# Two edits in an RWKV-7 block: group norm between the last sample states, and the inverse's levels in 32-column diagonal blocks

## Chip, cores and metric

One core of one Trainium2 chip, one launch. The metric is the device time of that launch in microseconds, lower is better. The program is written engine by engine in a low-level language: each engine has its own instruction queue, and the queues wait for each other by semaphores.

## The reference, cut to what matters

The model has two layers over 256 prompt rows and 8 x 4 sample rows (288 rows of 1024). Layer 0 is a gMLP block with a dense SwiGLU; layer 1 is an RWKV-7 time mixing with a mixture of experts (8 experts, top 2). The change lies in the time mixing. Its recurrence and its group norm:

```python
def step(s, inp):
    r_t, w_t, k_t, v_t, kk_t, a_t = inp
    s_kk = jnp.einsum("bhij,bhj->bhi", s, kk_t)
    s = (s * w_t[:, :, None, :]
         - s_kk[..., None] * (kk_t * a_t)[:, :, None, :]
         + v_t[..., None] * k_t[:, :, None, :])
    y = jnp.einsum("bhij,bhj->bhi", s, r_t)
    return s, y
...
yc = y - jnp.mean(y, axis=-1, keepdims=True)
y = yc * lax.rsqrt(jnp.mean(yc * yc, axis=-1, keepdims=True) + GN_EPS)
y = y.reshape(bsz, t, D_MODEL) * lnx_g + lnx_b
bonus = jnp.sum(rh * kh * r_k, axis=-1, keepdims=True) * vh
y = (y + bonus.reshape(bsz, t, D_MODEL)).astype(h.dtype)
out = (y * g) @ w_out
```

There are 16 heads of 64 columns. All of it is float32.

## The kernel before, in words

The recurrence over the prompt is done in four chunks of 64 rows. Inside a chunk the rows depend on each other by a unit triangular matrix of 64 x 64 for each head; its inverse is needed. Two chunks share the 128 partitions (chunk pair `i` = 0 or 1, the second chunk in partitions 64 to 127), so one step works on 2 x 16 matrices.

**The inverse** (queue steps `xt0`, `x0`, `t1`, `xl`) doubles its diagonal blocks: level 0 by a masked copy (L1162), then levels m = 1 to 5 for blocks of 2, 4, 8, 16 and 32. `XT` holds the transposed inverse so far, `X` the inverse. `t1` (TensorE L1663) multiplies the matrix `MS[.., BL, ..]` by X, ScalarE copies the product to `T1` (L808); `xl` (L1678) multiplies XT by T1 both ways round, and VectorE copies the entries of the level under a mask `lvl` into X and XT (L1170, copy_predicated). Level 5 updates only XT. Each step works in two halves `f` of eight heads; each half has 16 matmuls of 64x64 (8 heads, 2 chunks), and an fp32 matmul is two pairs of LDWEIGHTS and MATMUL in the trace. The two chunks' matmuls lie in different tiles of the array: rows and columns 0 to 63, and 64 to 127.

**The chunks** then run in order, `w1`, `u`, `s`, `y` for c = 0 to 3. In `u` TensorE multiplies the inverse by W1 (L1724) and puts `key_value` or `y_value` (L1711, L1716) between, which are of the same 64x64 shape:

```python
for p in range(DC):
    mm = t.matmul(banks[2 + h2][cs, 64 * p:64 * p + 64], XT[cs, i, 2 * p + h2, :], W1[cs, h2, p, :],
                  start=(p == 0), stop=True, skip_group_check=True)
    ...
    other(p, 1 - e)
```

**The samples** (8 sequences of 4 rows) have steps with a name in `q_`: scores (L1767), their small inverse in one 32x32 tile (L1779, L1786, L1793), `q_s0` (states in, L1807), `q_qs` (L1816, 8 moving columns), `q_w1`, `q_u` (L1828, L1832, L1840), `q_y`, and `q_st(p)` (L1865, L1874), which makes the new state of two heads and hands it to ScalarE (L854) and a DMA. For `q_st(p + 2)` GpSimd spreads keys into blocks (L611), after `q_st(p)`.

**The order** is written out by hand in one list `steps`, which every engine walks through: `then(step)` appends a step of the prompt and behind it the next one of `fill`, the list of sample steps and of the scores of the second chunk pair. When the prompt's steps are over, what is left of `fill` follows: here `q_u(1)`, `q_y(1)`, `q_st(4)` to `q_st(7)`.

**Group norm** comes after the list. TensorE transposes the prompt's last state for the output; then for each of 8 chunks of channels c a matmul with `halves` gives the mean (L1888), VectorE subtracts it (L1219), ScalarE squares (L860). Then for each c: the variance by `halves` (L1897), the gate's two matmuls with `b_g2` in banks 6 and 7 (L1901 with 128 rows, L1902 with 32), the square root on ScalarE (L863), and on VectorE reciprocal (L1223), times gain (L1225), plus `b_lnx_b` plus bonus (L1228), times gate (L1232). The output projection (L1913) waits for all eight.

Of the kernel before, what the change touches and what calls it, by code (L numbers as in the profile page):

```python
# [54 lines left out]
def trunk_kernel(nc, a, out):  # L55

    with ExitStack() as ctx:
# [113 lines left out]
        ysq = tokens(B[8])  # L171
# [5 lines left out]
        XT = view(B[0], 2 * D, "p (i h t) -> p i h t", i=2, h=H)  # L177
        X = view(B[0] + 2048, D, "p (h t) -> p h t", h=H)
        T1 = view(B[0] + 3072, D, "p (f h t) -> p f h t", f=2, h=8)
# [6 lines left out]
        lvl = view(CHN + 5376, 768, "p (l x t) -> p l x t", l=6, x=2)  # L186
# [6 lines left out]
        id64 = view(CHN + 7200, 64)  # L193
        mskS = view(CHN + 7424, 2 * SMP, "p (r t) -> p r t", parts=2 * SMP, r=2)
# [13 lines left out]
        wkvo = view(CHN + 1024, 512, "p (c j) -> p c j", c=DC)  # L208
# [31 lines left out]
        for name in """const pool_order vec_in x_in ws_in wsS_in router_in vec_ready tr_ready xt_ready sq_ready  # L240
# [7 lines left out]
            gn_root g_ready yg_ready wo_ready r_const zero_out outg_in r_logit r_chain r_exp r_e r_sel r_pos r_most xtk_dve  # L248
# [116 lines left out]
        steps += fill  # L365
# [40 lines left out]
        def x_count(i, m, f, x):  # L406

            return 18 * i + 4 * (m - 1) + (2 * f + x if m < 5 else f) + 1
# [41 lines left out]
        def _(sp):  # L450
# [24 lines left out]
            for st in steps:  # L475
                if st == ("xl", 1, 5):
                    sp.wait_ge(S["t1_ready"], 20)
# [49 lines left out]
        def _(pool):  # L527
# [60 lines left out]
            step(g.tensor_tensor(lvl, lvlW[:, :, :, 0:64], lvlW[:, :, :, 64:128], ALU.add))  # L588
            step(g.tensor_tensor(id64, ident[:, 0:64], ident[:, 64:128], ALU.add))

# [13 lines left out]
            g.tensor_copy(XT, bc(id64, 1, [P, 2 * H, 64]).rearrange("p (i h) t -> p i h t", i=2)).then_inc(S["masks"], 1)  # L604
            pool.wait_ge(S["masks"], 2)
            g.tensor_copy(XTq[SB], bc(id64[SB, SMP:2 * SMP], 1, [SMP, H, SMP])).then_inc(S["masks"], 1)
# [9 lines left out]
            pool.wait_ge(S["masks"], 3)  # L616
            pool.wait_ge(S["sc_ready"], 16)
# [15 lines left out]
            pool.wait_ge(S["st_tr"], 1)  # L633
# [10 lines left out]
            for i in range(3):  # L644
# [7 lines left out]
                .then_inc(S["outg_in"], 16)  # L652
            pool.wait_ge(S["zero_out"], 16)
# [27 lines left out]
        def _(act):  # L681
# [25 lines left out]
            act.dma_start(router, a["m_router"][0].rearrange("(k p) e -> p k e", p=P)).then_inc(S["router_in"], 16)  # L707
# [87 lines left out]
            for st in steps:  # L795
                k = st[0]
                if k == "x0":
                    i = st[1]
                    for f in range(2):
                        act.wait_ge(S["xt_tr"], 2 * i + f + 1)  # L800
                        s_.activation(X[:, 8 * f:8 * f + 8, :], banks[1 + 3 * f][:, :].rearrange("p (h t) -> p h t", h=8),
                                      ACT.Copy).then_inc(S["x0_ready"], 1)
                elif k == "t1":
                    _, i, m = st
                    n = 5 * i + m - 1
                    for f in range(2):
                        act.wait_ge(S["t1_ready"], 2 * n + f + 1)
                        s_.activation(T1[:, f], banks[3 * f][:, :].rearrange("p (h t) -> p h t", h=8), ACT.Copy) \  # L808
                            .then_inc(S["t1_done"], 1)
# [46 lines left out]
            act.wait_ge(S["st_tr"], 1)  # L856
            s_.activation(wkvo, banks[0][:, :].rearrange("p (c j) -> p c j", c=DC), ACT.Copy).then_inc(S["st_row"], 1)
            for c in range(DC):
                act.wait_ge(S["gn_yc"], c + 1)
                s_.activation(ysq[:, c, :], yT[:, c, :], ACT.Square).then_inc(S["gn_sq"], 1)  # L860
            for c in range(DC):
                act.wait_ge(S["gn_var"], c + 1)
                s_.activation(t1T[:, c, :], banks[4 + c % 2][:, 0:T], ACT.Sqrt, bias=eps[:, 2:3], scale=1.0 / HD) \  # L863
                    .then_inc(S["gn_root"], 1)
# [81 lines left out]
        def _(dve):  # L946
# [49 lines left out]
            dve.wait_ge(S["rows_in"], 48)  # L996
# [147 lines left out]
            for c in range(DC):  # L1144
                dve.wait_ge(S["rb_ready"], c + 1)
                v.tensor_tensor(bonT[:, c, :], banks[BON[c]][:, 0:T], vfT[:, c, :], ALU.mult).then_inc(S["bon_ready"], 1)
            for st in steps:
# [9 lines left out]
                elif k == "xt0":  # L1157
# [3 lines left out]
                    for f in range(2):  # L1161
                        v.copy_predicated(XT[:, i, 8 * f:8 * f + 8, :], bc(lvl[:, 0, 1, :], 1, [P, 8, 64]).bitcast(I32),  # L1162
                                          MS[:, BL, i, 8 * f:8 * f + 8, :]).then_inc(S["xt0_ready"], 1)
                elif k == "xl":
                    _, i, m = st
                    for f in range(2):
                        for x in range(0 if m < 5 else 1, 2):
                            dve.wait_ge(S["x_ready"], x_count(i, m, f, x))
                            dst = XT[:, i, 8 * f:8 * f + 8, :] if x else X[:, 8 * f:8 * f + 8, :]
                            v.copy_predicated(dst, bc(lvl[:, m, x, :], 1, [P, 8, 64]).bitcast(I32),  # L1170
                                              banks[1 + 3 * f + x][:, :].rearrange("p (h t) -> p h t", h=8)) \
# [30 lines left out]
                elif k == "q_xt0":  # L1202
                    q_wait(dve, "q_ms", 1)
                    v.copy_predicated(XTq[SB], bc(lvl[SB, 0, 1, SB], 1, [SMP, H, SMP]).bitcast(I32), MSq[SB, :, 0, :]) \
                        .then_inc(S["q_dve"], 1)
                elif k == "q_x2":
                    g_ = st[1]
                    q_wait(dve, "q_x2", g_)
                    v.copy_predicated(XTq[SB, 8 * g_:8 * g_ + 8, :], bc(lvl[SB, 1, 1, SB], 1, [SMP, 8, SMP]).bitcast(I32),
                                      banks[7][SB, 0:256].rearrange("p (h t) -> p h t", h=8)).then_inc(S["q_dve"], 1)  # L1210
                elif k == "q_y":
# [3 lines left out]
                                    Qs[:, :, 1, :], ALU.add).then_inc(S["q_dve"], 1)  # L1215

            for c in range(DC):
                dve.wait_ge(S["gn_mean"], c + 1)
                v.scalar_tensor_tensor(out=yT[:, c, :], in0=banks[2 + c % 2][:, 0:T], scalar=-1.0 / HD, in1=yT[:, c, :],  # L1219
                                       op0=ALU.mult, op1=ALU.add).then_inc(S["gn_yc"], 1)  # L1220
            for c in range(DC):
# [8 lines left out]
                dve.wait_ge(S["r_chain"], 3 * c + 3)  # L1230
                dve.wait_ge(S["g_ready"], c + 1)
                v.tensor_tensor(yT[:, c, :], banks[6 + c % 2][:, 0:T], yT[:, c, :], ALU.mult).then_inc(S["yg_ready"], 1)  # L1232
# [4 lines left out]
            chain = [3 * DC]  # L1237
# [157 lines left out]
        def _(pe):  # L1395
# [218 lines left out]
            BOTH = (slice(0, 64), slice(64, 128))  # L1614

# [9 lines left out]
            for st in steps:  # L1625
# [19 lines left out]
                elif k == "x0":  # L1645
                    i = st[1]
                    for f in range(2):
                        pe.wait_ge(S["xt0_ready"], 2 * i + f + 1)
                        for j in range(8):
                            for ch in BOTH:  # L1650
                                mm = t.matmul(banks[1 + 3 * f][ch, 64 * j:64 * j + 64], XT[ch, i, 8 * f + j, :], id64[ch],
                                              start=(j == 0), stop=True, skip_group_check=True)
                        mm.then_inc(S["xt_tr"], 1)
                elif k == "t1":
                    _, i, m = st
                    for f in range(2):
# [9 lines left out]
                elif k == "xl":  # L1666
                    _, i, m = st
                    for f in range(2):
                        pe.wait_ge(S["t1_done"], 2 * (5 * i + m - 1) + f + 1)
                        if m > 1:  # L1670
                            pe.wait_ge(S["x_done"], x_count(i, m - 1, f, 1))
                        elif i:
                            pe.wait_ge(S["x_done"], x_count(0, 5, f, 1))
                        for x in range(0 if m < 5 else 1, 2):
                            for j in range(8):
                                for ch in BOTH:
# [3 lines left out]
                            mm.then_inc(S["x_ready"], 1)  # L1680
                elif k == "w1":
# [3 lines left out]
                    if c == 0:  # L1685
                        pe.wait_ge(S["x_done"], 36)
# [381 lines left out]
```

## Time and profile before

| what | value |
|---|---|
| median of 3 runs | 1684.76 us (1683.76 to 1685.39) |
| the profiled execution | 1685.16 us, its span 1683.3 us |
| TensorE matmul busy | 1588.4 us (94% of the span) |
| VectorE, ScalarE, GpSimd busy | 1030.5, 780.3, 88.4 us |
| inverse, first x0 to last xl | 621 to 697 us |
| chunks of the prompt | 702 to 754 us |
| last sample states, group norm, gate | 757 to 811 us |

Times in the trace count from the span's start. PE is TensorE's matmuls, PEld its LDWEIGHTS, DVE VectorE, ACT ScalarE, POOL GpSimd, SP the queue of most DMAs. Busy time of PE is modelled to the matmul's end, so that neighbours overlap. "PEclk" is the granted clock of TensorE: 1.00 is 2.4 GHz, 0.50 is 1.2 GHz. A form like 64*32 is rows times columns of the stationary operand; "64x64" behind it is the moving one.

### The profile page before, as it was taken

The page shows a single profiled execution, that of the slowest core. Times are in us where ns is not written, and L with a number is a line of the kernel's source. Part 1 is how long each engine was busy: PE and PEld are TensorE (multiplying, and loading weights), DVE is VectorE, ACT ScalarE, POOL GpSimd, SP SyncE. Part 2 cuts the span into 40 slices and gives each one's busy share as a digit, 9 for nine tenths or more (in the row PEclk, how much of TensorE's full clock was granted, in tenths as well). Part 3 has the DMA queues.
Part 4 walks back from the last instruction along what each step waited for, and adds up shares of the span by engine and source line. Part 5 has one row for each costly group of instructions (what it writes and reads, how often), then busy time and mean ns, then how long its engine had stood idle before and what let it go on. Part 6 is the DMA issues. An engine that isn't in the chain of part 4 may idle for free.

```text
span 1683.3 us, 25991 instructions
## 1 busy us (share of the span) xinstructions
PE 1588.4 (94%) x11388; PEld 1258.0 (75%) x11388; DVE 1030.5 (61%) x981; ACT 780.3 (46%) x724; POOL 88.4 (5%) x140
## 2 busy tenths in 40 slices
PE   6999989999989999998869999999999999999991
PEld 5777769999957779995656777777777777777771
DVE  2243134544363645314357888888888888888883
ACT  1120034443331422222026777777777777777771
POOL 2300000000000001232000000000000000000001
PEclk9999999999989999986879999999999999999996
DMA  8443345545333220113039999999999999999963
GB/s 252 130 126 100 107 151 161 164 144 145 104 101 126 75 52 4 32 37 98 25 122 382 404 384 380 367 382 352 379 376 373 376 372 377 365 382 356 379 253 96
DMA packets 238282, 378.28 MB, mean 225 GB/s; under 512 B 27385, under 2 KB 141289, under 8 KB 226610
## 3 DMA queue, kind: packets, MB, share of 16 engines
q1 hardware_dynamic: 232370, 367.19, 62.5%
q0 software_dynamic: 2000, 6.04, 1.2%
q10 hardware_dynamic: 3792, 3.30, 0.6%
q8 instruction: 92, 1.51, 0.4%
q14 instruction: 28, 0.23, 0.0%
HBM read 368.34 MB, written 8.17 MB: 224 GB/s over the span
## 4 chain that ended last, share of the span: by engine, by line
PE 91%; DVE 5%; DMA 2%; issue 1%; ACT 1%; POOL 0%; ACTq 0%; POOLq 0%; DVEq 0%; SPq 0%
PE bank L1981 44%; PE bank L1486 13%; PE bank L1433 8%; PE bank L1532 6%; PE bank L1479 4%; PE bank L1913 2%; PE bank L1678 2%; PE bank L1991 1%; PE bank L1663 1%; PE bank L1470 1%; PE bank L1874 1%; DVE arena L336 1%; PE bank L1865 1%; PE bank L1922 0%; PE bank L1555 0%
## 5 line engine op out<-in xcount | busy, mean ns | idle before, releaser
L1285 DVE TENSOR_TENSOR wL<-ering,wH 128x2048 fp32r<-128x2048 f32 x264 | 604.4, 2290 | 100.1 <-ACT wH L882 95.0
L882 ACT ACTIVATE wH<-ering 128x2048 fp32r<-128x2048 f32 x264 | 506.0, 1917 | 154.9 <-PE bank L1981 154.8
L1981 PE MATMUL bank<-wH,xgH 128*96 128x512 f32 (+1 forms) x768 | 291.0, 379 | 1.2 <-DVE xgL L1292 1.2
L1981 PE MATMUL bank<-wH,xgL 128*96 128x512 f32 (+1 forms) x768 | 288.2, 375 | 0.0
L1981 PE MATMUL bank<-wL,xgH 128*96 128x512 f32 (+1 forms) x768 | 287.8, 375 | 0.0
L1981 PEld LDWEIGHTS bank<-wH,xgH 128*96 128x96 f32 x768 | 126.1, 164 | 44.1 <-DVE xgL L1292 1.5
L1981 PEld LDWEIGHTS bank<-wH,xgL 128*96 128x96 f32 x768 | 124.5, 162 | 44.8
L1981 PEld LDWEIGHTS bank<-wL,xgH 128*96 128x96 f32 x768 | 124.7, 162 | 42.4
L1981 PE MATMUL bank<-wH,hH 128*96 128x512 f32 x352 | 139.3, 396 | 0.0
L1981 PE MATMUL bank<-wH,hL 128*96 128x512 f32 x352 | 138.4, 393 | 0.0
L1981 PE MATMUL bank<-wL,hH 128*96 128x512 f32 x352 | 137.8, 392 | 0.0
L1433 PE MATMUL bank<-arena 128*128 128x288 f32 x512 | 129.4, 414 | 1.2 <-DVE arena L974 1.2
L1028 DVE TENSOR_TENSOR fwL<-fring,fwH 128x2048 fp32r<-128x2048 f32 (+1 forms) x38 | 76.3, 2011 | 80.7 <-ACT fwH L725 80.7
L1433 PEld LDWEIGHTS bank<-arena 128*128 128x128 f32 x512 | 98.4, 194 | 28.5 <-DVE arena L974 1.4
L1532 PE MATMUL bank<-arena 128*128 128x288 f32 (+2 forms) x448 | 112.6, 414 | 1.5 <-DVE arena L1081 1.5
L725 ACT ACTIVATE fwH<-fring 128x2048 fp32r<-128x2048 f32 (+1 forms) x38 | 64.0, 1684 | 104.9 <-DMA fring<-f_w_gate 60.7
L1486 PE MATMUL bank<-fxH,fwH 128*128 128x288 f32 x352 | 105.0, 298 | 7.0 <-DVE fxL L1036 7.0
L1532 PEld LDWEIGHTS bank<-arena 128*128 128x128 f32 (+2 forms) x448 | 82.8, 186 | 30.5 <-issue 4.3
L1486 PE MATMUL bank<-fxH,fwL 128*128 128x288 f32 x352 | 104.5, 297 | 0.0
L1486 PE MATMUL bank<-fxL,fwH 128*128 128x288 f32 x352 | 104.1, 296 | 0.0
L1981 PEld LDWEIGHTS bank<-wH,hL 128*96 128x96 f32 x352 | 56.7, 161 | 24.7
L1981 PEld LDWEIGHTS bank<-wL,hH 128*96 128x96 f32 x352 | 56.9, 162 | 23.0
(342 smaller groups left out, 2018.1 us busy)
## 6 DMA issues: line engine op xcount, KB each, us to landing
ering<-m_w_gate SPq DMA_DIRECT2D x88, 1024.0 KB, 7.7
ering<-m_w_up SPq DMA_DIRECT2D x88, 1024.0 KB, 8.3
ering<-m_w_down SPq DMA_DIRECT2D x88, 1024.0 KB, 7.6
arena<-a_w_in SPq DMA_DIRECT2D x16, 1024.0 KB, 5.4
arena<-b_w_rkv SPq DMA_DIRECT2D x12, 1024.0 KB, 5.1
fring<-f_w_gate SPq DMA_DIRECT2D x11, 1024.0 KB, 5.2
fring<-f_w_up SPq DMA_DIRECT2D x11, 1024.0 KB, 5.3
fring<-f_w_down SPq DMA_DIRECT2D x16, 704.0 KB, 4.7
```

Source lines behind the costliest of these rows:

```text
L336: nc.vector.scalar_tensor_tensor(out=dst[:, c, :], in0=xT[:, c, :], scalar=vec[:, gain + c:gain + c + 1], in1=rinv[:, :], op0=ALU.mult, op ...
L725: nc.scalar.activation(fwH[:, n % FRING, 0:w], fring[:, (F_GU + n) % RING, 0:w], ACT.Copy) \
L882: s_.activation(wH[:, g % HRING, :], ering[:, g % MRING, :], ACT.Copy).then_inc(S["e_hi"], 1)
L1028: v.tensor_tensor(fwL[:, n % FRING, 0:w], fring[:, (F_GU + n) % RING, 0:w], fwH[:, n % FRING, 0:w].bitcast(F32), ALU.subtract).then_inc(S[ ...
L1285: v.tensor_tensor(wL[:, g % HRING, :], ering[:, g % MRING, :], wH[:, g % HRING, :].bitcast(F32), ALU.subtract).then_inc(S["e_lo"], 1)
L1433: mm = t.matmul(banks[g_ % 4][:, 0:T], w[:, k, P * j:P * j + P], hT[:, k, :], start=(k == 0), stop=(k == DC - 1))
L1479: mm = t.matmul(banks[c % 4][:, 0:T], w[:, k, :], vT[:, k, :], start=(k == 0), stop=(k == AC - 1))
L1486: mm = t.matmul(bank[:, 0:T], w2[l], x2[r][:, k, :], start=(start and m == 0), stop=(stop and m == 2))
L1532: mm = t.matmul(bank, w(k), x[:, k, :], start=(k == 0), stop=(k == ks - 1))
L1678: mm = t.matmul(banks[1 + 3 * f + x][ch, 64 * j:64 * j + 64], pair[x], pair[1 - x], start=(j == 0), stop=True, skip_group_check=True)
L1913: mm = t.matmul(banks[c % 4][:, 0:T], w[:, k, P * j:P * j + P], yT[:, k, :], start=(k == 0), stop=(k == DC - 1))
L1981: mm = t.matmul(dst, lhs[l], rhs[r], start=(start and m == 0), stop=(stop and m == 2), skip_group_check=True)
```

## The change

**The inverse** keeps, for levels 0 to 4, only the diagonal blocks of 32 columns. XT, X, T1 and the masks `lvl` are 32 columns wide, and each 64x64 matmul becomes two of 32x32, so that a step has 32 matmuls a half in four tiles on the array's diagonal (`QUARTERS`). Level 0 takes four masked copies a pair instead of two. Level 5 makes the block below the diagonal: `t1` multiplies the lower left block of MS by X in the upper half, `xl` multiplies by T1 and copies XT through `id32`, both into bank 2, and one VectorE copy puts that into `XR`, the last 32 columns of XT for 64 rows. `u` multiplies the first 32 columns from XT (32 rows) and the last from XR (64 rows).

**Group norm** moves into the step list: `gm(c)` (mean, subtract, square) and `gv(c)` (variance, Ln on ScalarE) stand between `q_st(4)` to `q_st(7)`; then `state`, `gx` (eight Exp with scale -0.5 on ScalarE for the reciprocal root) and `gate(c)`. `b_lnx_b` is added to the bonus by GpSimd early (eight operations), and GpSimd adds the sum to yT before the gate; VectorE keeps the gain and the gate's product. The gate's matmuls use banks 0 and 1. `ysq` is a ring of four. The router's load shares a semaphore with other rows.

The core of the diff (masks' construction, views, wait counts and the sample inverse's `id64` to `id32` are left out):

```diff
-        steps += fill
+        while fill[0] != ("q_st", 4):
+            steps.append(fill.pop(0))
+        steps += [("gm", 0), ("gm", 1)]
+        for n in range(4):
+            steps += [fill.pop(0)] + [(k, 2 * n + j + 2 * (k == "gm")) for j in range(2) for k in ("gv", "gm") if k == "gv" or n < 3]
+        steps += [("state", 0), ("gx", 0)] + [("gate", c) for c in range(DC)]
...
+            pool.wait_ge(S["bon_ready"], DC)
+            for c in range(DC):
+                g.tensor_scalar(bonT[:, c, :], bonT[:, c, :], vcol("b_lnx_b", c), None, ALU.add).then_inc(S["gn_add"], 1)
...
+            for c in range(DC):
+                pool.wait_ge(S["r_chain"], c + 1)
+                g.tensor_tensor(yT[:, c, :], yT[:, c, :], bonT[:, c, :], ALU.add).then_inc(S["gn_add"], 1)
...
+                elif k == "gv":
+                    c = st[1]
+                    act.wait_ge(S["gn_var"], c + 1)
+                    s_.activation(rstd[:, c, :], banks[4 + c % 2][:, 0:T], ACT.Ln, bias=eps[:, 2:3], scale=1.0 / HD) \
...
+                elif k == "gx":
+                    act.wait_ge(S["gn_root"], DC)
+                    for c in range(DC):
+                        s_.activation(rstd[:, c, :], rstd[:, c, :], ACT.Exp, scale=-0.5).then_inc(S["gn_root"], 1)
...
-                    for f in range(2):
-                        v.copy_predicated(XT[:, i, 8 * f:8 * f + 8, :], bc(lvl[:, 0, 1, :], 1, [P, 8, 64]).bitcast(I32),
-                                          MS[:, BL, i, 8 * f:8 * f + 8, :]).then_inc(S["xt0_ready"], 1)
+                    for k4, rows in enumerate(QUARTERS):
+                        o = 32 * (k4 % 2)
+                        v.copy_predicated(XT[rows, i], bc(lvl[rows, 0, 1, :], 1, [32, H, 32]).bitcast(I32),
+                                          MS[rows, BL, i, :, o:o + 32]).then_inc(S["xt0_ready"], 1)
...
-            for c in range(DC):
-                dve.wait_ge(S["gn_root"], c + 1)
-                v.reciprocal(t1T[:, c, :], t1T[:, c, :]).then_inc(S["r_chain"], 1)
-                dve.wait_ge(S["r_chain"], 3 * c + 1)
-                v.scalar_tensor_tensor(out=yT[:, c, :], in0=yT[:, c, :], scalar=vcol("b_lnx_g", c), in1=t1T[:, c, :],
-                                       op0=ALU.mult, op1=ALU.mult).then_inc(S["r_chain"], 1)
-                dve.wait_ge(S["r_chain"], 3 * c + 2)
-                v.scalar_tensor_tensor(out=yT[:, c, :], in0=yT[:, c, :], scalar=vcol("b_lnx_b", c), in1=bonT[:, c, :],
-                                       op0=ALU.add, op1=ALU.add).then_inc(S["r_chain"], 1)
+                elif k == "gate":
+                    c = st[1]
+                    if c + 2 < DC:
+                        gn_scale(c + 2)
+                    dve.wait_ge(S["gn_add"], DC + c + 1)
+                    dve.wait_ge(S["g_ready"], c + 1)
+                    v.tensor_tensor(yT[:, c, :], banks[1 - c % 2][:, 0:T], yT[:, c, :], ALU.mult).then_inc(S["yg_ready"], 1)
...
-                            for ch in BOTH:
-                                mm = t.matmul(banks[3 * f][ch, 64 * j:64 * j + 64], MS[ch, BL, i, 8 * f + j, :], X[ch, 8 * f + j, :],
-                                              start=(j == 0), stop=True, skip_group_check=True)
+                            for k4, rows in enumerate(QUARTERS):
+                                o = 32 * (k4 % 2)
+                                mm = t.matmul(banks[3 * f][rows, 32 * j:32 * j + 32], MS[rows, BL, i, 8 * f + j, o:o + 32],
+                                              X[rows, 8 * f + j, :], start=(j == 0), stop=True, skip_group_check=True)
...
-                                for ch in BOTH:
-                                    pair = (XT[ch, i, 8 * f + j, :], T1[ch, f, j, :])
-                                    mm = t.matmul(banks[1 + 3 * f + x][ch, 64 * j:64 * j + 64], pair[x], pair[1 - x],
+                                for rows in QUARTERS:
+                                    pair = (XT[rows, i, 8 * f + j, :], T1[rows, 8 * f + j, :])
+                                    mm = t.matmul(banks[1 + 3 * f + x][rows, 32 * j:32 * j + 32], pair[x], pair[1 - x],
                                                   start=(j == 0), stop=True, skip_group_check=True)
...
+                    for j in range(H):
+                        for lhs, to in ((T1, 0), (id32, 32)):
+                            for ch in (0, 64):
+                                rows = slice(ch + 32, ch + 64)
+                                mm = t.matmul(banks[2][ch + to:ch + to + 32, 32 * j:32 * j + 32],
+                                              lhs[rows, j, :] if to == 0 else lhs[rows], XT[rows, i, j, :],
+                                              start=(j == 0), stop=True, skip_group_check=True)
...
-                            mm = t.matmul(banks[2 + h2][cs, 64 * p:64 * p + 64], XT[cs, i, 2 * p + h2, :], W1[cs, h2, p, :],
+                            lo, hi = slice(64 * e, 64 * e + 32), slice(64 * e + 32, 64 * e + 64)
+                            t.matmul(banks[2 + h2][lo, 64 * p:64 * p + 64], XT[lo, i, 2 * p + h2, :], W1[lo, h2, p, :],
+                                     start=(p == 0), stop=True, skip_group_check=True)
+                            mm = t.matmul(banks[2 + h2][hi, 64 * p:64 * p + 64], XR[cs, i, 2 * p + h2, :], W1[cs, h2, p, :],
                                           start=(p == 0), stop=True, skip_group_check=True)
```

## Rows read from the trace of the kernel before

**Rows 1.** The page's chain that ended last, shares of the span by engine.

```profile
PE 91%; DVE 5%; DMA 2%; issue 1%; ACT 1%; POOL 0%; ACTq 0%; POOLq 0%; DVEq 0%; SPq 0%
```

**Rows 2.** The chain of waits in the inverse: start us, us, what, instructions.

```profile
655.18 1.87 PE bank L1663 x64
657.04 0.62 PE bank L1786 x16
657.66 2.01 PE bank L1678 x64
```

**Rows 3.** Windows: length, busy us by engine, PEclk, DMA share, GB/s.

```profile
core 0: us, PE busy (x) PEld busy (x) DVE busy (x) ACT busy (x) POOL busy (x), PEclk, DMA share, GB/s
655.00:670.00 15.00, 15.00 (x496) 14.71 (x492) 4.30 (x8) 5.75 (x10) 0.00 (x0) 1.00 0.02 5
738.00:742.00 4.00, 4.00 (x96) 4.00 (x96) 0.69 (x1) 0.59 (x1) 1.04 (x1) 0.60 0.02 4
776.00:785.00 9.00, 8.05 (x27) 4.11 (x26) 5.45 (x10) 6.21 (x12) 2.33 (x7) 1.00 0.31 88
785.00:811.00 26.00, 20.20 (x35) 8.99 (x36) 24.85 (x31) 2.50 (x5) 0.00 (x0) 0.51 0.13 41
```

**Rows 4.** Windows of L1767's loads alone (sample scores, form 64*32): loads begun.

```profile
618.00:618.08 0.08, 0.06 (x8) 1.00 1.21 221
618.00:618.19 0.19, 0.17 (x16) 1.00 1.18 210
```

**Rows 5.** Timeline, PEld, of three steps: start us, us, line, forms, count.

```profile
614.34 3.51 PEld L1640 LDWEIGHTS bank<-arena 64*64 64x64 f32 x128 [1.07 <-issue]
...
662.40 0.57 PEld L1793 LDWEIGHTS bank<-arena 32*32 32x32 f32 x16
...
694.23 1.02 PEld L1816 LDWEIGHTS bank<-arena 64*64 64x64 f32 x32
```

**Rows 6.** Loads around changes of form; first one line's durations in ns.

```profile
L1828 PEld LDWEIGHTS bank<-arena x32: 101/105/105, 697.2 to 747.8; 32*32 32x32 f32 x32
...
697.18 0.91 PEld L1828 LDWEIGHTS bank<-arena 32*32 32x32 f32 x16
698.19 0.79 PEld L1832 LDWEIGHTS bank<-ident,arena 128*32 128x32 f32 x8
...
780.97 0.29 PEld L1902 LDWEIGHTS bank<-arena 32*128 32x128 f32 x2 [0.39 <-issue]
781.65 0.30 PEld L1897 LDWEIGHTS bank<-arena,halves 128*128 128x128 f32 x2 [0.39 <-issue]
...
787.75 0.50 PEld L1902 LDWEIGHTS bank<-arena 32*128 32x128 f32 x2 [0.76 <-issue]
789.01 0.50 PEld L1897 LDWEIGHTS bank<-arena,halves 128*128 128x128 f32 x2 [0.76 <-issue]
```

**Rows 7.** Timeline, PEld, inside u(2).

```profile
729.48 0.19 PEld L1711 LDWEIGHTS bank<-arena 64*64 64x64 f32 x2
729.54 0.19 PEld L1724 LDWEIGHTS bank<-arena 64*64 64x64 f32 x2
```

**Rows 8.** Timeline of group norm's stretch, one row of each kind.

```profile
753.60 0.60 ACT L823 ACTIVATE arena<-bank 128x512 f32<-128x512 f32 x1 [3.02 <-PE bank L1757]
...
761.07 7.80 POOL L611 TENSOR_TENSOR arena<-arena 32x1024 f32<-32x1024 f32 x4 [13.76 <-PE bank L1874]
...
781.06 1.28 ACT L863 ACT_TABLE_LOAD   x1
...
789.82 1.94 DVE L1223 RECIPROCAL arena<-arena 128x288 f32<-128x288 f32 x1
...
791.79 0.52 DVE L1225 SCALAR_TENSOR_TENSOR arena<-arena,vec 128x288 f32<-128x288 f32 x1
...
792.90 0.46 DVE L1232 TENSOR_TENSOR arena<-bank,arena 128x288 f32<-128x288 f32 x1
...
810.75 34.01 PE L1913 MATMUL bank<-arena 128*128 128x288 f32 x128 [4.31 <-issue]
```

**Rows 9.** Timeline, VectorE: the copies of xt0 for the second pair.

```profile
641.75 3.60 DVE L1162 COPY_PREDICATED arena<-arena 128x512 f32<-128x512 int32 x2
```

More of the change, by code:

```diff
@@ L207, in trunk_kernel @@
         SB = slice(SMP, 2 * SMP)
-        wkvo = view(CHN + 1024, 512, "p (c j) -> p c j", c=DC)
+        QUARTERS = [slice(32 * k, 32 * k + 32) for k in range(4)]
+        wkvo = view(CHN + 1024 + 4 * T, 512, "p (c j) -> p c j", c=DC)
         h3T = tokens(B[8])
@@ L1236, in _ @@
             norm_dve(3, col["norm_ffn_g"] + 8, tokens(B[8]))
-            chain = [3 * DC]
+            chain = [DC]
             def link(ins):
@@ L1646, in _ @@
                     i = st[1]
+                    pe.wait_ge(S["xt0_ready"], 4 * i + 4)
                     for f in range(2):
-                        pe.wait_ge(S["xt0_ready"], 2 * i + f + 1)
                         for j in range(8):
-                            for ch in BOTH:
-                                mm = t.matmul(banks[1 + 3 * f][ch, 64 * j:64 * j + 64], XT[ch, i, 8 * f + j, :], id64[ch],
+                            for rows in QUARTERS:
+                                mm = t.matmul(banks[1 + 3 * f][rows, 32 * j:32 * j + 32], XT[rows, i, 8 * f + j, :], id32[rows],
                                               start=(j == 0), stop=True, skip_group_check=True)
                         mm.then_inc(S["xt_tr"], 1)
-                elif k == "t1":
+                elif k == "t1" and st[2] < 5:
                     _, i, m = st
@@ L1876, in _ @@
                     mm.then_inc(S["q_pe"], 1)
-            pe.wait_ge(S["s_done"], 4)
-            for p in range(DC):
-                for ch in BOTH:
-                    mm = t.matmul(banks[0][ch, 64 * p:64 * p + 64], St[ch, 0, p, :], id64[ch],
-                                  start=(p == 0), stop=True, skip_group_check=True)
-            mm.then_inc(S["st_tr"], 1)
-            pe.wait_ge(S["y_done"], 4)
-            q_wait(pe, "q_yc", 1)
-            for c in range(DC):
-                if c >= 2:
-                    pe.wait_ge(S["gn_yc"], c - 1)
-                t.matmul(banks[2 + c % 2][:, 0:T], halves[:, :], yT[:, c, :], start=True, stop=True) \
-                    .then_inc(S["gn_mean"], 1)
@@ L1890, in _ @@
-            s_ = arrived()
-            g2v = (slot(s_, None, n=D), slot(s_, None, parts=LG - P, n=D, off=D))
-            q_wait(pe, "q_so", DC - 1)
-            for c in range(DC):
-                pe.wait_ge(S["gn_sq"], c + 1)
-                if c >= 2:
-                    pe.wait_ge(S["gn_root"], c - 1)
-                t.matmul(banks[4 + c % 2][:, 0:T], halves[:, :], ysq[:, c, :], start=True, stop=True) \
-                    .then_inc(S["gn_var"], 1)
-                if c >= 2:
-                    pe.wait_ge(S["yg_ready"], c - 1)
-                t.matmul(banks[6 + c % 2][:, 0:T], g2v[0][:, P * c:P * c + P], lg1[:, 0, :], start=True, stop=False)
-                t.matmul(banks[6 + c % 2][:, 0:T], g2v[1][:, P * c:P * c + P], lg1[0:LG - P, 1, :], start=False, stop=True) \
-                    .then_inc(S["g_ready"], 1)
+                elif k == "gm":
+                    c = st[1]
+                    if c == 0:
+                        pe.wait_ge(S["y_done"], 4)
+                        q_wait(pe, "q_yc", 1)
+                    elif c >= 2:
+                        pe.wait_ge(S["gn_yc"], c - 1)
+                    t.matmul(banks[2 + c % 2][:, 0:T], halves[:, :], yT[:, c, :], start=True, stop=True) \
+                        .then_inc(S["gn_mean"], 1)
+                elif k == "gv":
+                    c = st[1]
+                    if c == 0:
+                        pe.wait_ge(S["s_done"], 4)
+                    elif c >= 2:
+                        pe.wait_ge(S["gn_root"], c - 1)
+                    pe.wait_ge(S["gn_sq"], c + 1)
+                    t.matmul(banks[4 + c % 2][:, 0:T], halves[:, :], ysq[:, c % 4, :], start=True, stop=True) \
+                        .then_inc(S["gn_var"], 1)
+                elif k == "state":
+                    pe.wait_ge(S["s_done"], 4)
+                    for p in range(DC):
+                        for ch in BOTH:
+                            mm = t.matmul(banks[0][ch, 64 * p:64 * p + 64], St[ch, 0, p, :], id64[ch],
+                                          start=(p == 0), stop=True, skip_group_check=True)
+                    mm.then_inc(S["st_tr"], 1)
+                elif k == "gate":
+                    c = st[1]
+                    if c == 0:
+                        s_ = arrived()
+                        g2v = (slot(s_, None, n=D), slot(s_, None, parts=LG - P, n=D, off=D))
+                    elif c == 1:
+                        pe.wait_ge(S["st_row"], 1)
+                    else:
+                        pe.wait_ge(S["yg_ready"], c - 1)
+                    bank = banks[1 - c % 2][:, 0:T]
+                    t.matmul(bank, g2v[0][:, P * c:P * c + P], lg1[:, 0, :], start=True, stop=False)
+                    t.matmul(bank, g2v[1][:, P * c:P * c + P], lg1[0:LG - P, 1, :], start=False, stop=True) \
+                        .then_inc(S["g_ready"], 1)
```

132 lines of the change are left out of this document (82 added, 50 removed).

## The prediction

> **What bounds the kernel now.** I read the page first. Its chain of waits is 91% TensorE [rows 1], so a microsecond taken from or put on TensorE's queue counts in full wherever it is not waiting. The change touches three stretches: the inverse (620 to 697 us), the four chunks (702 to 754 us), and the last sample states with group norm (757 to 811 us). I read the chain of the inverse next [rows 2]: nothing but TensorE pieces end to end. One level is t1 (1.87 to 2.01 us), a fill step (0.9 to 1.0 [rows 5]), xl (twice t1) and another fill, 7.3 us together. ScalarE and VectorE, which copy and select between them, are covered by the fills. The windows say that TensorE is busy for all of 655 to 670 us at the full clock, and that the clock falls to half later [rows 3]: at 738 us after two steps of 8-column matmuls, and for all of 785 to 811 us. A matmul in fp32 is two pairs of LDWEIGHTS and MATMUL (64 pairs for the 32 matmuls of t1). Group norm goes at 3.47 us a chunk of channels, from one reciprocal to the next: 1.94 + 0.52 + 0.52 + 0.46 us on VectorE (one of the two of 0.52 is shown [rows 8]), with three pairs of matmuls beside it that take as long at half clock. It is 57.2 us from the end of y(3), where ScalarE copies its result (753.60), to the first matmul of the output projection (810.75) [rows 8].
>
> **Part 1, the levels.** Each 64x64 matmul becomes two of 32x32: 384 pairs a level instead of 192. Before, a pair costs 29 ns (1.87 / 64). What is that limit? The q_qs steps take 1.02 us for 32 pairs (28.7 ns apart, taking the 0.13 us of the last off) with only 8 columns moving, so it is the load of 64 columns in a tile, about 57 ns, shared by two tiles. A lone 32x32 tile takes 29 ns a pair (16 in 0.57 us) [rows 5]. So four 32x32 tiles could take 29 / 4 = 7.3 ns a pair, if the pairs can be issued so fast. No row shows that for long. The low bound: the scores of the samples start 8 loads in 60 ns and then 16 in 170 ns [rows 4], 7 to 11 ns, but only 32 pairs and after a queue had filled. The high bound: 128 pairs of the scores in 3.51 us [rows 5], 27 ns, which is the longest fast run. At 7.3 ns a level has 2.8 us of pairs instead of 5.6; with two fills, their mode changes (part 2) and the copies, which are then exposed, I get about 5 us instead of 7.3. Over the second pass (4 levels, x0 and level 5, which loses 1.7 us) that is 12 us. In the first pass VectorE holds it: it multiplies scores there, and xt(1) is now four copies instead of two, in a stretch where two took 3.60 us beside GpSimd [rows 9]; I give it 5 us. xt(0) costs two copies more, 1.4 us. Best: 17 us less. At 27 ns: (384 x 27 - 5600) ns = +4.8 us a level, eight levels, plus 4 for x0 and the fifth level: 42 us more, less what the loads would hide: +40. I take 14 ns, the middle in ratio of 7 and 27: 5.4 us a level, level 5 a microsecond shorter, the mode changes 0.3 us each way: -3 us in all. Copies and selections become half as long; they stay beside TensorE.
>
> The Trainium skill (TensorEngine Tiling (Array Packing), Instruction Overhead) puts about 60 cycles on each matmul however few columns move, and advises against taking a tiling factor from a dimension that is already small. By it a level would have 384 x 25 = 9.6 us of pairs, 4 us more than now, near my high bound; the burst of rows 4 starts faster than that rule allows, so I leave it as a rival.
>
> **Part 2, u.** This is where I see the cost. u used to be, for each p and h2, one 64x64 matmul and one key_value or y_value of the same shape: two tiles, 58 ns from one LDWEIGHTS pair to the next [rows 7], 0.115 us for both, 16 times, 1.85 us a chunk. After the change each of the 16 has three forms in turn: 32x32 (XT), 64x32 (XR), 64x64 (key_value or y_value). What does a change of form cost? The last of 16 loads of form 32*32 starts at 697.18 + 0.91 less its own 0.105, at 697.99 us, and the next form's first load at 698.19 [rows 6]: 0.20 us, against 0.03 to 0.06 within a form. The same between 128 and 32 rows: the load of L1902 starts at 780.97 and that of L1897 at 781.65, 0.68 us for two matmul passes of 288 columns, which stream 0.48 us; so +0.20. In rows 2 the change shows as 0.62 us for 16 pairs that need 0.47. So one fp32 matmul alone in its form takes 0.05 us to its second pass and 0.20 us to the next load: 0.25 us, three of them 0.75 us, 16 times: 12.0 us. That is +10.2 us a chunk, **+41 us** in all at the full clock. Nothing covers it: y, s and w1 wait for u.
>
> The clock makes it worse. In u TensorE would stream 0.107 of each 0.25 us. The stretch 776 to 785 us, better filled than that, was followed (after some 2 us of idle) by half clock; so were two q_qs steps (734 to 738) [rows 3]. At half clock the lone step costs 1.26 us for 0.96 us of streaming [rows 6], so +0.30; a lone 64-column matmul then takes 0.45 us, three of them 1.35. If the full clock lasts some 4 us of each u (five of 16 rounds), a u takes 3.8 + 11 x 1.35 = 18.7 us: +16.8 a chunk, +67 us. The steps behind it stand at half clock until it rises: 738 to 742 us is such a stretch [rows 3], 4 us of wall for 2 of work, though some of the work after 735 us is at half clock already. I take **+70 us** for the chunks. Bounds: +41 (full clock throughout), and about +105 if the chunks run at half clock from end to end (21.6 - 1.85 for u, and 7 us for the rest, four times).
>
> **Part 3, states and group norm.** Removed: eight reciprocals (1.94 us) and the addition of b_lnx_b and the bonus (0.52) from VectorE; per chunk of channels there remain 0.52 + 0.46 us. Added: eight Exp on ScalarE (about 0.5 us each, below the 0.60 of 512 elements, only the first exposed) with a table load of 1.28 us [rows 8] in front; an addition on GpSimd per chunk, 0.6 us by the row of L611 (1.95 us for 1024 elements a lane), beside VectorE's multiplication of the next. GpSimd's eight additions of b_lnx_b lie in 615 to 621 us, where it was idle. Mean and variance (16 x 2 passes) go between the q_st steps, where the state of p+2 waits for GpSimd's blocks (7.80 us after q_st(4) [rows 8]). At full clock I follow it so: q_y ends as now (757.2), q_st(4) 761, q_st(5) 765.2, q_st(6) 769.5, q_st(7) 773.7 (each 2 us, with 2.1 us of group norm behind it), state 776, first Exp 778.4; then 1.36 us a chunk on TensorE (two lone forms of 0.68) for the gate: output projection from 789, 21.5 us sooner. At half clock throughout each q_st is 4 and each group 4.1 us, the gate 2.5 us a chunk: 813, 2.6 us later. The gate's part (785 to 811) stands at half clock now [rows 3]; I take -12 us. The router's semaphore, the mask's three additions and the changed layouts change nothing on the path.
>
> **Sum.** The profiled execution took 1685.16 us (span 1683.3), 0.4 above the median of the runs. 1685.2 - 3 + 70 - 12 = 1740.2, against the median 1739.8: **1740 us**.
>
> **Rivals.**
> A. The clock stays up through u. For it: TensorE never waits long there, only 0.15 us at a time. Against it: the fall at 738 us. It gives +41, with it a good inverse (-10) and -18 behind: 1698 us. Still slower. 14%.
> B. The forms of u do not drain (the two 32-column forms count as one, or loads pass each other). Then a round has six pairs at 28.7 ns, 0.17 us instead of 0.115, +4 us in all; with -6 for the inverse and -17 for group norm: 1666 us. It decides as long as u adds less than the 15 us that the other parts bring, 0.23 us to each of 64 rounds: under 0.35 us a round, half of the 0.75 that the rows give. For it: no row has 32*32 beside 64*32, or a form that changes after every matmul of 64 columns. 11%.
> C. Issue of the small pairs is slow, 25 to 27 ns: +40 instead of -3 and the rest as forecast: 1783 us. For it: no long run is faster. Against: rows 4. 12%.
> D. All small gains meet small costs and nothing moves: 3%.
> Forecast 60%.
>
> **Range and chances.** The forecast's own range is 1705 to 1775. Down to A and up to C: 1690 to 1790 leaves B (11%) and a few per cent above. Within 0.2% (3.4 us, about what a measurement of this kernel can tell from no change): 3%; faster: 12% (B, and the best corner of A); slower: 85%.
>
> **What would show it.** In the changed trace: u(0) to u(3) take 12 to 22 us each instead of 1.9, with their LDWEIGHTS about 0.20 us behind the one before wherever the form changes, and granted clock 0.5 in them; a level takes 5 to 8 us, and its LDWEIGHTS say by their spacing whether 7, 14 or 27 ns a pair holds; no reciprocal in group norm, the output projection 14 us nearer to y(3)'s end. I am wrong if u's rounds take under 0.4 us, or if the levels take over 10 us.

## The result, and the profile after

The changed kernel takes 1792.4 us (median of 4 runs, 1789.1 to 1796.7) against 1684.3 us before: ratio 1.0646, 95% interval 1.0618 to 1.0675. It is slower, as forecast, but by 108 us and not by 55: outside the range, by 2 us. The profiled execution took 1789.1 us, its span 1787.2.

The stages by their first and last TensorE instruction in the two traces:

| stage | before | after | difference | forecast |
|---|---|---|---|---|
| first score to end of inverse | 614.37 to 697.25 | 615.40 to 744.86 | +46.6 | -3 |
| first u to end of y(3) | 702.20 to 753.56 | 751.36 to 871.16 | +68.4 | +70 |
| end of y(3) to output projection | 753.56 to 810.75 | 871.16 to 916.96 | -11.4 | -12 |
| all the rest | | | +0.3 | 0 |

In two of three parts the sum came out as forecast. In the inverse it did not. Its chain of waits after, over one level of the second pair (start us, us, what, instructions), answers to [rows 2]:

```profile
696.21 2.49 issue
698.70 1.33 PE bank L1720 x83
...
700.84 0.37 PE bank L1705 x22
701.22 0.94 issue
702.16 1.60 PE bank L1705 x101
703.76 1.68 PE bank L1872 x27
...
706.11 1.84 PE bank L1720 x123
707.94 1.24 issue
709.18 2.01 PE bank L1720 x127
711.19 1.82 issue
```

L1705 is t1, L1720 xl, L1872 and L1881 are fills. Before there was TensorE work end to end; now "issue" stands between the pieces, time in which TensorE waited for nothing that the profile shows. It is 28% of the chain from 650 to 750 us. No copy and no selection ends such a gap. A level takes 12.3 to 13.3 us (t1 starts at 688.20, 700.45, 713.74 and 726.99 us) instead of 7.3.

The timeline of the weight loads shows the same as bursts:

```profile
706.03 1.77 PEld L1720 LDWEIGHTS bank<-arena 32*32 32x32 f32 x123
709.18 1.87 PEld L1720 LDWEIGHTS bank<-arena 32*32 32x32 f32 x128 [1.37 <-issue]
713.01 0.13 PEld L1720 LDWEIGHTS bank<-arena 32*32 32x32 f32 x3 [1.96 <-issue]
```

Inside a burst a pair of LDWEIGHTS and MATMUL takes 14 ns (1.77 us for 123), which is the very figure that I had taken, though here at half clock. But from the start of a burst to the start of the next it is 3.1 to 3.8 us. The DMA part of the page has a queue that I had not read, that of the instructions. From 692 to 730 us:

```profile
GB/s 17 0 0 0 17 0 0 0 17 0 0 0 17 0 0 17 0 0 0 17 0 0 0 17 0 0 0 17 0 0 0 17 0 0 0 17 0 0 0 17
...
q8 instruction: 11, 0.18, 2.0%
```

Eleven packets of 16 KB in 38 us, one every third or fourth slice of 0.95 us: 3.7 us from one to the next. A burst of 128 pairs is 256 instructions, 64 bytes each if one packet holds them. The pages of the two whole runs bear that out: the changed kernel has 29846 instructions and 107 such packets, the kernel before 25991 and 92, so 15 packets more for 3855 instructions more, 64 bytes each.

The windows answer to [rows 3]; in u the loads answer to [rows 7], first at the full clock, then at half:

```profile
core 0: us, PE busy (x) PEld busy (x) DVE busy (x) ACT busy (x) POOL busy (x), PEclk, DMA share, GB/s
650.00:750.00 100.00, 73.06 (x3368) 68.02 (x3370) 23.65 (x37) 11.42 (x26) 12.76 (x8) 0.54 0.04 11
751.40:756.00 4.60, 4.60 (x45) 2.96 (x42) 0.00 (x0) 0.59 (x1) 0.00 (x0) 0.99 0.02 4
756.00:785.00 29.00, 29.00 (x342) 22.09 (x340) 2.36 (x4) 3.19 (x6) 7.57 (x4) 0.53 0.09 19
```

```profile
751.36 0.13 PEld L1787 LDWEIGHTS bank<-arena 32*32 32x32 f32 x2
...
751.60 0.13 PEld L1789 LDWEIGHTS bank<-arena 64*32 64x32 f32 x2
751.83 0.19 PEld L1773 LDWEIGHTS bank<-arena 64*64 64x64 f32 x2
752.08 0.13 PEld L1787 LDWEIGHTS bank<-arena 32*32 32x32 f32 x2
...
759.79 0.17 PEld L1787 LDWEIGHTS bank<-arena 32*32 32x32 f32 x2
760.14 0.18 PEld L1789 LDWEIGHTS bank<-arena 64*32 64x32 f32 x2 [0.17 <-issue]
760.49 0.28 PEld L1778 LDWEIGHTS bank<-arena 64*64 64x64 f32 x2 [0.17 <-issue]
760.89 0.17 PEld L1787 LDWEIGHTS bank<-arena 32*32 32x32 f32 x2
```

L1787 is the 32x32 matmul of u with XT, L1789 the 64x32 one with XR, L1773 and L1778 are key_value and y_value. A round of three forms takes 0.72 us at the full clock (forecast 0.75) and 1.10 us at half (forecast 1.35). The four u take 14.66, 14.20, 15.36 and 16.00 us instead of some 2.05 each, +52 us; the steps between them, which stand at 0.50 to 0.84 of the full clock, take the other 16 us. In group norm, against [rows 8]:

```profile
897.75 1.28 ACT L895 ACT_TABLE_LOAD   x1
899.04 2.77 ACT L895 ACTIVATE arena<-arena 128x288 f32<-128x288 f32 x8
...
911.38 0.46 DVE L1271 TENSOR_TENSOR arena<-bank,arena 128x288 f32<-128x288 f32 x1 [1.63 <-PE bank L1978]
913.89 0.46 DVE L1271 TENSOR_TENSOR arena<-bank,arena 128x288 f32<-128x288 f32 x1 [2.06 <-PE bank L1978]
```

The reciprocals are gone. Each of the last chunks takes 2.51 us (911.38 to 913.89), in which VectorE waits 2.06 us for the gate's matmuls (L1977 and L1978, two forms, at half clock): the forecast had 2.5 us a chunk.

### The profile page after: what moved, and what is told of

It is laid out like the page before. It is cut to its first block, busy times and chain, and to the rows that moved or that the text cites. A ratio compares the mean times of both kernels' runs of the same rounds, so it can differ in the third digit from the quotient of the medians.

```text
span 1787.2 us, 29846 instructions
## 1 busy us (share of the span) xinstructions
PE 1660.5 (93%) x13308; PEld 1302.9 (73%) x13308; DVE 1007.2 (56%) x967; ACT 779.6 (44%) x732; POOL 102.6 (6%) x159
## 4 chain that ended last, share of the span: by engine, by line
PE 91%; DVE 4%; issue 3%; DMA 1%; ACT 0%; POOL 0%; ACTq 0%; POOLq 0%; DVEq 0%; SPq 0%
PE bank L2057 41%; PE bank L1526 12%; PE bank L1473 7%; PE bank L1572 5%; PE bank L1519 4%; PE bank L1989 2%; PE bank L1720 2%; PE bank L1789 1%; PE bank L2067 1%; PE bank L1787 1%; PE bank L1773 1%; PE bank L1705 1%; PE bank L1510 1%; PE bank L1778 1%; PE bank L1872 1%
## 5 line engine op out<-in xcount | busy, mean ns | idle before, releaser
L1473 PEld LDWEIGHTS bank<-arena 128*128 128x128 f32 x512 | 97.4, 192 | 27.9 <-DVE arena L1005 1.4
```

The costliest lines, as they stand in the source:

```text
L1473: mm = t.matmul(banks[g_ % 4][:, 0:T], w[:, k, P * j:P * j + P], hT[:, k, :], start=(k == 0), stop=(k == DC - 1))
```

## The experiments

Theory I for the inverse: instructions reach TensorE in blocks of 256, one in 3.6 to 3.7 us; whatever needs more than one pair each 28 to 30 ns runs dry once the queue is empty. Rival II: the small tiles or the half clock hold each pair. Rival III: the copies and selections do. For u: the changes of form, against the mere number of matmuls or the clock.

**bench**: what a pair costs by itself (one run).

```diff
             pe.wait_ge(S["bon_ready"], DC)
+            fill_queue()
+            for n in range(96):
+                for r in Q4:
+                    t.matmul(b7[r, 0:32], ident[r, 0:32], ident[r, 32:64], start=True, stop=True, skip_group_check=True)
+            fill_queue()
...
```

> This is the kernel before with dummy matmuls in front of the scores (they write to a PSUM bank that the scores overwrite later; nothing is left out). Each block stands behind 8 dense matmuls of 288 columns. Blocks: 384 fp32 matmuls on four 32x32 tiles in turn with 32 columns; 256 with 8 columns; 192 on two 64x64 tiles with 64 columns and 192 with 8; 128 on the whole array with 32 columns; 128 on a single 32x32 tile; then 16 rounds each of the forms 32x32, 64x32, 64x64 in turn, of 32x32 and 64x32, of 64x32 and 64x64, and of 64x64 on the two tiles of one form; at last 384 bf16 matmuls (one pass each) on four 32x32 tiles. Theory I (instructions arrive in blocks of 16 KB, 256 instructions, each some 3.6 us): after a quick start every long block settles at 28 to 30 ns for a pair of LDWEIGHTS and MATMUL, with 8 columns as with 32, on four tiles as on one, in bf16 as in fp32 (bf16 matmuls then come twice as often). Rival II (tile and clock): four 32x32 tiles with 8 columns are quicker than with 32, 7 to 14 ns against 14 to 29, and the single tile is the slowest of all. Forms: 0.20 us from the last load of one form to the first of the next at full clock, so a round of three forms 0.7 us, of two 0.45 to 0.5, and two tiles of one form 0.12; the rival for the forms (it is the number of matmuls) says 0.17 for three.

The loads of the first block (four 32x32 tiles, 32 columns), on the timeline:

```profile
617.87 1.58 PEld L1625 LDWEIGHTS bank<-ident 32*32 32x32 f32 x177 [0.39 <-issue]
622.74 1.16 PEld L1625 LDWEIGHTS bank<-ident 32*32 32x32 f32 x128 [3.29 <-issue]
626.48 1.79 PEld L1625 LDWEIGHTS bank<-ident 32*32 32x32 f32 x128 [2.58 <-issue]
630.22 1.80 PEld L1625 LDWEIGHTS bank<-ident 32*32 32x32 f32 x128 [1.94 <-issue]
634.23 1.79 PEld L1625 LDWEIGHTS bank<-ident 32*32 32x32 f32 x128 [2.21 <-issue]
637.97 1.15 PEld L1625 LDWEIGHTS bank<-ident 32*32 32x32 f32 x79 [1.95 <-issue]
```

That is the cleanest picture of it. The 177 pairs that were waiting go at 9 ns each; then come bursts of 128, whose starts lie 3.74 us apart (one 4.01), with no other engine at work. Other DMA traffic was heavy until about 625 us; from 625.5 to 639 us the queues moved only three instruction packets, 3.7 us apart, and the bursts kept their distance. 3.74 us for 128 pairs is 29.2 ns a pair. The table of lines gives the other blocks (busy us, mean ns; then idle time before):

```profile
L1637 PEld LDWEIGHTS bank<-ident 64*64 64x64 f32 x384 | 17.4, 193 | 0.4 <-issue 0.4
L1633 PEld LDWEIGHTS bank<-ident 64*64 64x64 f32 x384 | 11.3, 135 | 0.4 <-issue 0.4
L1643 PEld LDWEIGHTS bank<-ident 32*32 32x32 f32 x256 | 9.9, 121 | 0.4 <-issue 0.4
L1625 PEld LDWEIGHTS bank<-ident 32*32 32x32 f32 x768 | 9.3, 132 | 12.4 <-issue 12.4
L1629 PEld LDWEIGHTS bank<-ident 32*32 32x32 f32 x512 | 6.0, 130 | 6.3 <-issue 6.3
...
L1665 PEld LDWEIGHTS bank<-ident 32*32 32x32 bf16 x384 | 3.3, 91 | 5.7 <-issue 5.7
```

Busy and idle over the count: four tiles 28 ns with 32 columns (L1625) and 24 with 8 (L1629, the queued pairs of the start included), bf16 23 ns (L1665, of 384 pairs 241 went before the first gap). Neither the columns nor half the bytes change the distance of the blocks much: the starts lie 3.74 and 3.46 us apart with 8 columns and 4.00 us in the one interval of bf16. Two 64x64 tiles with 64 columns take 29.4 ns a pair without any gap, at the full clock throughout (L1633). With 8 columns (L1637) the first 127 pairs take 29.1 ns at the full clock, the others 52 ns at half. The first pairs of both blocks were waiting already and still go at 29 ns, not at 9, so this is the tiles' own rate; it equals the supply, and the kernel before never showed the supply. A single 32x32 tile takes 31.5 ns at the full clock; the expectation that it too would settle at 28 to 30 was not met, its pairs follow each other without a gap, so it is bound by the tile (48 ns at the half clock later). The rounds of three forms take 0.71 us (775.76 to 776.47 us, first loads), those of two 0.45 (32x32 and 64x32) and 0.48 (64x32 and 64x64) at the full clock, 0.69 and 0.75 at half, and 64x64 on two tiles 0.115.

**level_half**: is it the supply in the kernel too? Half of the blocks' matmuls are left out, so only the stretch of the inverse is read (one run).

```diff
-                            for k4, rows in enumerate(QUARTERS):
+                            for k4, rows in ((0, QUARTERS[0]), (2, QUARTERS[2])):
...
-                                for rows in QUARTERS:
+                                for rows in QUARTERS[0::2]:
```

> The changed kernel with only two of the four 32x32 tiles at work in x0 and in levels 1 to 4 of the inverse (rows 0 to 31 and 64 to 95; half of the blocks are left out, so only the stretch of the inverse is read, not the total). Each tile that still works does the same matmuls as before, copies and selections are as they were, and the number of pairs of a level falls from 384 to 192. Theory I (supply of instructions, some 29 ns a pair, with the 64 pairs of the fills about 256 pairs): a level falls from 12.5 to 13.3 us to 7.3 to 8 us, and the inverse ends 38 to 46 us sooner. Rival II (a tile takes its time, or the half clock does): a level stays above 11 us. Rival III (copies and selections on ScalarE and VectorE hold it): a level stays above 11 us with idle time put down to them. If the fast start of four tiles (8 ns a pair) were what counts, it would be below 6 us.

The chain of waits over one level:

```profile
691.57 3.55 PE bank L1720 x128
695.12 1.81 PE bank L1881 x32
696.93 1.69 PE bank L1705 x58
```

A level takes 7.6 us (xl of 684.02 and of 691.57 us), no "issue" among its pieces, and the inverse ends at 710.0 instead of 744.9 us. With half of the matmuls and everything else in place the excess is gone but for the half clock: the window 650 to 700 us has it at 0.50, and the 128 pairs of two tiles take 27.7 ns each there. The instruction packets lie 4.1 us apart here (four in 690 to 706 us), slower than they can come. Rivals II and III, by which a level had to stay above 11 us, fall. The inverse ended 34 us sooner (counted from the scores), a little less than I expected: at half clock two tiles are themselves near the rate of the supply.

**u_grouped**: the same matmuls of u, ordered by form.

```diff
                             t.matmul(banks[2 + h2][lo, 64 * p:64 * p + 64], XT[lo, i, 2 * p + h2, :], W1[lo, h2, p, :],
                                      start=(p == 0), stop=True, skip_group_check=True)
+                        for p in range(DC):
                             mm = t.matmul(banks[2 + h2][hi, 64 * p:64 * p + 64], XR[cs, i, 2 * p + h2, :], W1[cs, h2, p, :],
                                           start=(p == 0), stop=True, skip_group_check=True)
...
+                        for p in range(DC):
                             other(p, 1 - e)
```

> The changed kernel with the same matmuls of u in another order: all eight 32x32 of a parity, then all eight 64x32, then the eight of key_value or y_value. If the changes of form cost the time (6 in a u instead of 48), a u takes 4 to 5.5 us instead of 14.2 to 16, the chunks 76 to 83 us instead of 120, and the kernel 1752 us (1745 to 1760). If it is the number of matmuls or the clock that costs, a u stays above 12 us and the kernel above 1780.

1760.7 us, ratio to before 1.0453 (1.0420 to 1.0486), 32 us less than the changed kernel. The chain in u(0), where L1790 is now the matmul with XR:

```profile
752.19 0.76 PE bank L1787 x14
752.95 1.01 PE bank L1790 x16
753.96 1.51 PE bank L1773 x16
755.47 1.84 PE bank L1787 x16
757.31 1.84 PE bank L1790 x16
```

The u take 7.3, 5.2, 6.0 and 6.9 us, the chunks 88.7 us (751.87 to 840.59). Grouping takes 35 us off the 52 that u itself had grown by, so the changes of form, with the clock that came with them, cost the larger part of u (the mean clock is 0.67, 1.00, 0.85 and 0.71 in these four u, 0.57 to 0.69 in the changed kernel). For the chunks it gives 31 of 68 us back, not the 37 to 44 that I expected; the chunks, three of the four u and, narrowly, the time lie above the expected ranges. What I had left out shows in the rows: eight matmuls in turn on one tile don't overlap, 63 ns a load at the full clock and 115 at half, and the half clock is back at 755.5 us.

**u_full**: the blocks put together to 64x64 again.

```diff
+                        for lo in (slice(0, 32), slice(64, 96)):
+                            v.tensor_copy(XF[lo, i, :, 0:32], XT[lo, i]).then_inc(S["masks"], 1)
...
+                            mm = t.matmul(banks[2 + h2][cs, 64 * p:64 * p + 64], XF[cs, i, 2 * p + h2, :], W1[cs, h2, p, :],
+                                          start=(p == 0), stop=True, skip_group_check=True)
```

> The changed kernel, except that the inverse's blocks are put together into 64x64 again (two copies and the result of level 5 beside them) and u is one 64x64 matmul for each head, as before. If all that the chunks lost comes from the new forms, a u is back at 2.0 to 2.2 us, the chunks at 51 to 53 us, and the kernel takes 1724 us (1720 to 1730), with the inverse still 45 to 48 us longer than before. If the chunks suffer from the half clock that the inverse leaves, they stay above 60 us.

1725.9 us, ratio 1.0234 (1.0203 to 1.0265). The u take 2.03 to 2.08 us and the chunks 51.4 us (759.29 to 810.66), to the tenth what they were before, although the inverse ahead of them stood near half clock as in the changed kernel (0.56 and 0.54 over 650 to 750 us). The 68 us of the chunks are the new forms and what they do to the clock; nothing comes from the inverse. The inverse itself takes 133.9 us from the first score, 51 more than before (expected 45 to 48) and 4.4 more than in the changed kernel; whether that is the copies I did not test.

**gn_only**: the third part alone, with inverse and u of before.

```diff
-        steps += fill
+        while fill[0] != ("q_st", 4):
+            steps.append(fill.pop(0))
+        steps += [("gm", 0), ("gm", 1)]
...
```

> The kernel before with group norm and the last steps as changed, and the inverse and u as they were. If the parts add up: the stretch from the end of y(3) to the output projection loses 11 to 13 us as in the changed kernel, everything ahead of it stays within 1 us, and the time is 1672 us (1669 to 1675), ratio to before 0.993. Rival: what group norm gives depends on the half clock that u had left behind; entered at another clock it gives 4 us or less, or more than 16.

1672.4 us, ratio 0.9927 (0.9905 to 0.9949). From the end of y(3) (752.35) to the output projection (798.15) it is 45.8 us, as in the changed kernel. What lies ahead of it is 1.2 us shorter than in the kernel before, where I expected less than 1 us either way. That part is good by itself, and its gain does not depend on what stands before it.

**gn_gate**: the rule of u applied to the gate.

```diff
+                    for c in range(DC):
+                        t.matmul(banks[GATE[c]][:, 0:T], g2v[0][:, P * c:P * c + P], lg1[:, 0, :], start=True, stop=False)
+                    for c in range(DC):
+                        t.matmul(banks[GATE[c]][:, 0:T], g2v[1][:, P * c:P * c + P], lg1[0:LG - P, 1, :], start=False, stop=True)
```

> The run gn_only with the gate's matmuls grouped by form: all eight of 128 rows, then all eight of 32 rows, into eight banks, ahead of the Exp, instead of the two forms in turn for each chunk of channels (15 changes of form become 1, and nothing on TensorE waits for VectorE there). What then remains behind the Exp is VectorE's 1.16 us a chunk (0.70 + 0.46). Expected: output projection 5 to 9 us sooner than in gn_only (790 to 793 us instead of 798), time 1665 us (1662 to 1669). Rival: VectorE beside GpSimd's additions is the bound either way; then less than 2 us is won.

The end of the chain before the output projection, first of gn_only (L1938 and L1939 the gate's two forms, L1950 the projection), then of gn_gate (L1938, L1940 and L1951):

```profile
794.96 1.26 PE bank L1938 x2
796.22 1.25 PE bank L1939 x2
797.48 0.67 issue
798.15 2.26 PE bank L1950 x4
```

```profile
779.01 4.08 PE bank L1938 x16
783.09 4.07 PE bank L1940 x16
787.16 4.12 issue
791.28 8.87 PE bank L1951 x28
```

Thirty-two passes in 8.2 us, at the full clock, instead of 2.5 us for every four at half. The projection starts at 791.3 us. The profile puts the 4.12 us before it down to nothing ("issue"), but VectorE's last product of the gate ends at 791.18 us, and the projection waits for all eight of them. 1666.0 us, ratio 0.9891 (0.9873 to 0.9909): this version beats both kernels, by 17 and by 126 us.

## Why the prediction was wrong, point by point

**Part 1, the failed step.** "I take 14 ns, the middle in ratio of 7 and 27 ... -3 us in all." Measured: +46.6 us. Both bounds were real: 8.4 ns in a burst at the full clock, 29 ns for anything longer than the queue holds. But they are no ends of one scale, so their middle is no estimate. The low one holds for the pairs that were queued while TensorE did something slow; the high one for a level, 384 pairs and 48 or 64 of fills: 432 or 448 x 29.2 = 12.6 or 13.1 us, against 12.3 to 13.3 measured. It holds for the whole inverse: from the first x0 to its end there are 4228 pairs in 119.7 us, 28.3 ns each, where the kernel before had 2433 in 76.0 us, 31.2 ns each. The term that had to be taken was that of rival C, "Issue of the small pairs is slow, 25 to 27 ns", at 12%. Its +40 us is near; what it lacks is 29 ns instead of 27, and x0(0), which waits for four copies instead of one (its first matmul is 9.8 us behind the first score instead of 6.9: +2.9 us where I had 1.4). The prediction's own sign of being wrong, a level over 10 us, came true. The measured terms of all parts close the sum: 1685.2 + 46.6 + 68.4 - 11.4 + 0.3 = 1789.1, the profiled execution; the median of the runs is 3.3 above it. The rows before held the sign: 128 pairs at 27 ns next to 8 at 7 ns meant a queue, as I wrote, and a queue has a refill rate, which I did not ask for. L1640 and t1 could not show it: with two 64x64 tiles the tiles' own rate, which I read there, and the supply lie too close together, at 27 to 29 ns. The Trainium skill's floor for a matmul (TensorEngine Tiling (Array Packing), Instruction Overhead, about 60 cycles, by my estimate 25 ns at 2.4 GHz) lies between the two: the runs go below it in bursts and stay above it for long.

**Part 1, clock.** I left the half clock out of the inverse. It is there (0.54 over 650 to 750 us, with TensorE busy 73% of the time), and with it a burst takes 1.8 us instead of 1.2. It costs little, since the next block of instructions isn't there yet: the supply alone accounts for a level.

**Part 2, u.** The mechanism was right: 0.20 us from form to form, a round 0.72 us at the full clock, and the clock falls. That the sum came out at +68.4 us against +70 is partly luck, since two terms missed by 15 and 13 us in opposite ways: u itself +52 (forecast +67), because a round at half clock takes 1.10 us and not 1.35; the steps between, which I had at 3, +16. No row stood behind the "some 4 us" of full clock in each u; the first u had about 4.6, and the mean clock of the four was 0.66, 0.69, 0.61 and 0.57. Rival B (forms that don't drain) is refuted by the loads of u and by the bench; rival A (the clock stays up) by the windows: it fell after some 4.6 us of the first u.

**Part 3.** The sum was right: -11.4 against -12, and the same in gn_only. Two of its terms missed and nearly cancel. The first Exp comes 27.9 us behind the end of y(3) and not 24.8, the stretch standing at 0.79 of the full clock and not at all of it; from there to the projection it is 17.9 us and not eight times 2.5, because the first chunks take 1.0 and 1.5 us. The 2.5 us a chunk of the gate, taken as given, was changes of form and clock and could be removed (gn_gate). GpSimd's additions took 0.93 us where I had 0.6 (five in 4.65 us), and VectorE's multiplications 0.64 to 0.88 beside them instead of 0.52; from the third chunk on both are hidden, since VectorE waits for the gate's matmuls there.

## What to carry to other kernels

Splitting matmuls into smaller tiles multiplies instructions: count pairs, and multiply by the rate at which new blocks of them arrive (here 29 ns a pair) before counting what the array could do. Two tiles of 64x64 already use that rate, so four of 32x32 have nothing to gain in a long stretch. Where matmuls of several forms alternate, each alone in its form, order them by form: every change costs 0.20 us here at the full clock, and in these stretches the clock fell to half as well.

## What the runs showed of the hardware that I had not expected

- Instructions come to TensorE in blocks of 256, mostly 3.74 us apart in bench, with the DMA queues otherwise idle; after slow work some 160 to 240 pairs are in stock (161, 177 and 241 before the first gap) and go at 8 to 9 ns each.
- The distance of the blocks hardly depends on columns or type (3.46 and 3.74 us with 8 columns, 4.00 us in the one interval of bf16). Why it is 3.7 us, when the packet itself is 16 KB, was not settled; the runs only show that no other traffic is needed for it.
